# Stage borders of a two-layer decoder trunk: embedding, sums of squares, next layer's x, first loads

## What is computed

```
x += 1/2 * SwiGLU(RMSNorm(x))                        # ffn1, inner width 2816
x += W_out [ NSA | DiffAttn | HGRN2 ](RMSNorm(x) @ W_in)
x += 1/2 * SwiGLU(RMSNorm(x))                        # ffn2
x += sigmoid(RMSNorm(x) @ W_g) * RMSNorm(p[i] @ W_p) # p: per-layer embedding, width 256
SwiGLU(h) = (silu(h @ w_gate) * (h @ w_up)) @ w_down
```

## Time and profile before

| | us |
|---|---|
| median of 3 runs | 2407.98 |
| lowest, highest | 2405.62, 2409.56 |
| profiled execution | 2406.93 |
| its span, first to last instruction | 2405.1 |
| TensorE busy in it | 2292.6 |
| VectorE, ScalarE, GpSimd busy | 1208.7, 901.8, 82.5 |

### The profile page before, as it was taken

The page is one execution under the profiler, slowest core; times in us unless marked ns, Lnnn a source line. Parts: engine busy times, 40 slices in busy tenths (PEclk is TensorE's granted clock), DMA queues, the critical chain, the costliest instruction groups (busy, mean ns, idle before and its releaser), DMA issues. The chain is left out here.

```text
span 2405.1 us, 27598 instructions
## 1 busy us (share of the span) xinstructions
PE 2292.6 (95%) x10816; PEld 1806.7 (75%) x10816; DVE 1208.7 (50%) x1990; ACT 901.8 (37%) x1483; POOL 82.5 (3%) x119
## 2 busy tenths in 40 slices
PE   7999999899989999998989999998989899999988
PEld 5888887776656888887768888877766568888876
DVE  5444433466676444433554443345566764444335
ACT  5222223444654323222452322244455542222233
POOL 0000000032000000000000000001310000000000
PEclk9999999999999999999999999999999999999999
DMA  4433334212102333333223333343120023333322
GB/s 154 146 96 97 90 98 152 87 60 65 42 27 72 96 103 91 93 99 105 79 78 97 96 95 97 98 132 100 53 77 27 25 81 98 97 97 98 98 94 70
DMA packets 68986, 214.31 MB, mean 89 GB/s; under 512 B 8143, under 2 KB 15311, under 8 KB 68858
## 3 DMA queue, kind: packets, MB, share of 16 engines
q1 hardware_dynamic: 59344, 189.27, 26.1%
q10 hardware_dynamic: 9514, 23.27, 2.9%
HBM read 208.30 MB, written 5.40 MB: 89 GB/s over the span
## 5 line engine op out<-in xcount | busy, mean ns | idle before, releaser
L501 PE MATMUL main<-xh,wh 128*128 128x512 f32 x1944 | 781.5, 402 | 20.9 <-DVE xl L1407 19.7
L502 PE MATMUL main<-xl,wh 128*128 128x512 f32 x1944 | 763.2, 393 | 0.0
L503 PE MATMUL main<-xh,wl 128*128 128x512 f32 x1944 | 763.0, 392 | 0.0
L1400 DVE TENSOR_TENSOR wl<-raw,wh 128x1024 fp32r<-128x1024 f32 (+3 forms) x372 | 440.2, 1184 | 402.7 <-ACT wh L948 402.2
L948 ACT ACTIVATE wh<-raw 128x1024 fp32r<-128x1024 f32 (+3 forms) x372 | 378.1, 1017 | 499.6 <-PE main L503 465.4
L501 PEld LDWEIGHTS main<-xh,wh 128*128 128x128 f32 x1944 | 368.9, 190 | 128.0 <-issue 25.8
L502 PEld LDWEIGHTS main<-xl,wh 128*128 128x128 f32 x1944 | 369.1, 190 | 78.9 <-issue 5.5
L503 PEld LDWEIGHTS main<-xh,wl 128*128 128x128 f32 x1944 | 368.7, 190 | 78.6
L501 PE MATMUL main<-ffh,wh 128*128 128x512 f32 x704 | 273.9, 389 | 0.0
L502 PE MATMUL main<-ffl,wh 128*128 128x512 f32 x704 | 273.9, 389 | 0.0
L503 PE MATMUL main<-ffh,wl 128*128 128x512 f32 x704 | 273.9, 389 | 0.0
(11 more groups left out here) (230 smaller groups left out, 1937.8 us busy)
## 6 DMA issues: line engine op xcount, KB each, us to landing
raw<-in_ffn_gate SPq DMA_DIRECT2D x88, 512.0 KB, 3.6
raw<-in_ffn_up SPq DMA_DIRECT2D x88, 512.0 KB, 3.6
raw<-in_ffn_down SPq DMA_DIRECT2D x64, 448.0 KB, 3.3
raw<-in_w_in_t SPq DMA_DIRECT2D x40, 512.0 KB, 3.6
raw<-in_ffn_down SPq DMA_DIRECT2D x32, 512.0 KB, 3.5
raw<-in_wout SPq DMA_DIRECT2D x24, 384.0 KB, 3.1
w<-in_cmp_w ACTq DMA_DIRECT2D x16, 512.0 KB, 3.7
raw<-in_ple_gate SPq DMA_DIRECT2D x16, 512.0 KB, 3.2
```

The lines of the kernel that those rows point to most:

```text
L501: nc.tensor.matmul(out, lh, rh, start=start, stop=False, **kw)
L502: nc.tensor.matmul(out, lh, rl, start=False, stop=False, **kw)
L503: return nc.tensor.matmul(out, ll, rh, start=False, stop=stop, **kw)
L1400: nc.vector.tensor_tensor(wl[:, c % SLOTS, 0:n], raw[:, c % SLOTS, 0:n], wh[:, c % SLOTS, 0:n], ALU.subtract).then_inc(*tick("weights_lo", ...
```

## The change

1. The embedding is loaded into the FFN's gate buffer `fg` behind the last SiLU of ffn2, and is split during down product 3; its split form moves behind the FFN's buffers.
2. In both FFNs the sum of squares moves behind up product 0; one more chunk is split in tile 0, on ScalarE ahead of the factor.
3. "post" moves behind gate product 0 of the embedding stage; factor "ple" moves on ScalarE between output tiles 3 and 4; VectorE multiplies `emby` tile by tile within the loop over gate products.
4. In layer 0 the next layer's x is split tile by tile as the last gate product has read it (`x_read`): tiles 0 to 4 behind gate tile 6, tiles 5 to 7 behind gate tile 7.
5. At the start weight chunk 0 is loaded ahead of the table, the parameters behind chunk 2, and the line is copied behind tile 3.

```diff
@@ memory @@
+        embh, embl = sb("embh", [P, 2, SEQ], F32R), sb("embl", [P, 2, SEQ], F32R)
+        emb = fg
         place["at"] = region + (P - region) % 2048
-        emb = sb("emb", [P, 2, SEQ])
-        embh, embl = sb("embh", [P, 2, SEQ], F32R), sb("embl", [P, 2, SEQ], F32R)
@@ SyncE @@
-                sp.dma_start(onehot[0:33, :], a["onehot"]).then_inc(onehot_in, 16)
-                sp.dma_start(tab[0:BUCKETS, :], a["rel_bias"]).then_inc(onehot_in, 16)
...
                 load_ends(0)
-                load_params(0)
...
+                    if c == 0:
+                        sp.dma_start(onehot[0:33, :], a["onehot"]).then_inc(onehot_in, 16)
+                        sp.dma_start(tab[0:BUCKETS, :], a["rel_bias"]).then_inc(onehot_in, 16)
+                    if c == 2:
+                        load_params(0)
@@ TensorE @@
+                        if read and k < KT - 1:
+                            mm.then_inc(*tick("x_read", k))
...
+                        from_x((name + "_up", ft))
                         if ft == 0:
                             sum_squares(name)
-                        from_x((name + "_up", ft))
...
-                        sum_squares(("ple", "post")[h2])
+                        if h2 == 0:
+                            sum_squares("ple")
                     for dt in range(KT):
-                        from_x(("ple_gate", dt), "ple" if dt == 0 else None)
+                        from_x(("ple_gate", dt), "ple" if dt == 0 else None, read=dt == KT - 1 and layer < DEPTH - 1)
+                        if dt == 0:
+                            sum_squares("post")
@@ ScalarE, ffn @@
                             split(c + AHEAD)
                             if ft == 0:
+                                split(c + 1 + AHEAD)
                                 factor(name, rb[:])
...
+                    if name == "ffn2":
+
+                        act.dma_start(emb[:], a["p"][counts.layer]).then_inc(emb_in, 16)
                     for dt in range(KT):
...
                         square(nxt, dt, x[:, dt, :])
+                        if name == "ffn2" and dt == 3:
+                            act.wait_ge(emb_in, 16 * (counts.layer + 1))
+                            for k in range(2):
+                                nc.scalar.activation(embh[:, k, :], emb[:, k, :],
+                                                     ACT.Copy).then_inc(*tick("emb_hi", k))
@@ ScalarE, layers @@
+                def next_x(ks):
+
+                    counts.layer += 1
+                    for k in ks:
+                        if k < KT - 1:
+                            act.wait_ge(*done("x_read", k, layer=counts.layer - 1))
+                        else:
+                            act.wait_ge(*done("product", ("ple_gate", KT - 1), layer=counts.layer - 1))
+                        act.wait_ge(*done("x_new", "ple", k, layer=counts.layer - 1))
+                        split_x("ffn1", "ffn1", k)
+                    counts.layer -= 1
...
                     for dt in range(KT):
                         if dt % 4 == 0:
                             split(CHUNK[("ple_proj", dt // 4)] + AHEAD)
+                        if dt == 4:
+                            factor("ple", rb[:])
...
+                    split(CHUNK[("ple_gate", 0)] + AHEAD)
                     factor("post", rb2[:])
+                    if layer < DEPTH - 1:
+                        act.wait_ge(ends_in[layer + 1], 48)
                     for dt in range(KT):
                         split(CHUNK[("ple_gate", dt)] + AHEAD)
-                        if dt == 0:
-                            factor("ple", rb[:])
                         act.wait_ge(*done("pgate_scaled", dt))
                         nc.scalar.activation(pg[:, dt % 2, :], pg[:, dt % 2, :],
                                              ACT.Sigmoid).then_inc(*tick("pgate", dt))
+                        if layer < DEPTH - 1 and dt >= KT - 2:
+                            next_x(range(0, 5) if dt == KT - 2 else range(5, KT))
@@ VectorE @@
-                            split(c + AHEAD)
+                            split(c + AHEAD + (ft == 0))
...
-                    dve.wait_ge(*done("factor", "post"))
-                    for dt in range(KT):
-                        nc.vector.scalar_tensor_tensor(out=emby[:, dt, :], in0=emby[:, dt, :], scalar=col("post", dt),
-                                                       in1=rb2[:], op0=ALU.mult,
-                                                       op1=ALU.mult).then_inc(*tick("emb_normed", dt))
...
                         nc.vector.tensor_tensor(pg[:, dt % 2, :], bank_of(("ple_gate", dt))[:], rb[:],
                                                 ALU.mult).then_inc(*tick("pgate_scaled", dt, frees=("ple_gate", dt)))
+                        if dt == 0:
+                            dve.wait_ge(*done("factor", "post"))
+                        nc.vector.scalar_tensor_tensor(out=emby[:, dt, :], in0=emby[:, dt, :], scalar=col("post", dt),
+                                                       in1=rb2[:], op0=ALU.mult,
+                                                       op1=ALU.mult).then_inc(*tick("emb_normed", dt))
...
+                        if layer < DEPTH - 1 and dt >= KT - 2:
+                            next_x(range(0, 5) if dt == KT - 2 else range(5, KT))
```

More of the change, by code:

```diff
@@ L508, in chunk, with from_x @@
                     return wh[:, c % SLOTS, 0:n], wl[:, c % SLOTS, 0:n]
-                def from_x(key, stage=None, at=None, order=tuple(range(KT))):
+                def from_x(key, stage=None, at=None, order=tuple(range(KT)), read=False):
                     out = take(key, 0, at)
@@ L1344, in _ @@
                     at["logs"] = False
[L1345 to L1351, removed]
+                    if layer == 0:
+                        act.wait_ge(ends_in[layer], 48)
+                        for k in range(KT):
                             act.wait_ge(x_in[k], 16)
-                        split_x("ffn1", "ffn1", k)
-                        if k < AHEAD:
-                            split(k)
+                            split_x("ffn1", "ffn1", k)
+                            if k < AHEAD:
+                                split(k)
                     split(AHEAD)
@@ L1364, in _ @@
                     ffn("ffn2", "ple", "ple")
[L1366 to L1369, removed]
                     for dt in range(KT):
@@ L1521, in ffn @@
                         add_square(nxt, dt)
+                        if name == "ffn2" and dt == 3:
+                            for k in range(2):
+                                dve.wait_ge(*done("emb_hi", k))
+                                nc.vector.tensor_tensor(embl[:, k, :], emb[:, k, :], embh[:, k, :],
+                                                        ALU.subtract).then_inc(*tick("emb_lo", k))
                 def scaled(name, out):
@@ L1914, in mixed_lo, with next_x @@
                                             ALU.subtract).then_inc(*tick("x_lo", "mixed", k))
+                def next_x(ks):
+                    counts.layer += 1
+                    for k in ks:
+                        split_x("ffn1", "ffn1", k)
+                    counts.layer -= 1
                 for layer in range(DEPTH):
                     counts.layer = layer
[L1918 to L1927, removed]
+                    if layer == 0:
+                        for k in range(KT):
+                            if k < AHEAD:
+                                split(k)
+                            split_x("ffn1", "ffn1", k)
+                            if k == 3:
+                                dve.wait_ge(line_made, 1)
+                                nc.vector.tensor_copy(line[0:BIAS_HEADS, 0:SEQ],
+                                                      bank_of("line0")[0:BIAS_HEADS, :]).then_inc(
+                                                          *tick("line_copied", 0, frees="line0"))
+                                nc.vector.tensor_copy(line[0:BIAS_HEADS, SEQ:LINE],
+                                                      bank_of("line1")[0:BIAS_HEADS, 0:P]).then_inc(
+                                                          *tick("line_copied", 1, frees="line1"))
                     split(AHEAD)
@@ L1936, in _ @@
                     ffn("ffn2", "ple", "ple")
[L1937 to L1940, removed]
                     for dt in range(KT):
```

## The result

The changed kernel takes 2366.67 us (median of 4 runs, 2365.19 to 2371.97), the kernel before 2408.77 beside it (2405.62 to 2411.61): ratio 0.9828, 95% interval 0.9815 to 0.9842. The forecast was 2370.6 in a range of 2364 to 2379. Its profiled execution took 2371.97 us, of which 2370.2 span.

What follows compares the result with a forecast made beforehand. TensorE was taken to bound all but some 50 us, at the borders; gains of 6.5 (start), 11.2 and 11.7 (embedding borders) and 8.0 (layer border) sum to 37.4, giving 2370.6 us, range 2364 to 2379.

Steps and rivals of the forecast that it cites:

- the embedding border: End of second FFN to first embedding-gate product, twice: 19.7 us warm, 20.4 with clock; gains 11.2 and 11.7 us.
- the new stall: Embedding border: TensorE waits 1.7 us before gate product 0 for the bank freed by ScalarE's copy of output tile 4.
- The hidden part: Embedding border: the squares of "post" end at 1153.8, behind gate product 0 until 1154.55, hidden by 0.7 us.
- The table load: ScalarE, factor "ple" at the embedding border: load costs 1.28 us, without the skill page's added drain of about 1.38 us.
- Layer border: Layer 0's end to layer 1's first up product: 15.3 us against 23.37, gain 8.0, with stalls of 2.2 and 1.1 us.
- The wait for acc: Layer border: TensorE stalls 1.1 us behind the up product until the additions of squares end.
- The start: First gate matmul to the sum of squares' end: 29.9 against 36.43 us, gain 6.5, ends 4 and 8.5.
- I take 0.4 us off it: The start: weight chunk 1, landing at 13.43 before, is taken to land 0.4 us earlier.
- FFN entries: Squares behind the up product at four entries: the later factor is covered; second FFN's two entries gain 0.
- rival D: Slower than before: lag after FFN entries delays weights in 84 gate-up pairs; 2421 us at 0.6 us each; chance 0.03.
- C: Short stalls keep the clock low, 2.3 us at each of three places, start at its low end: 2378.3 us; chance 0.15.
- B: No new stalls at the embedding and layer borders: 2360.7 us, about 2364 with one of them left; chance 0.12.

Runs made afterwards that it cites:

- The two undone versions: Changed kernel with the embedding loaded and split only after ffn2: 2386.77 us; changed kernel with squares "post" back ahead of gate product 0: 2376.99 us.
- the second profile: The changed kernel run again unaltered, beside the kernel with three further edits: median 2370.34 us, profiled execution 2364.24 us.
- the version with three more edits: Changed kernel with factor ple behind the embedding output's squares, layer 0's chunk 1 behind all x tiles, layer 1's behind the early tiles: 2366.29 us.
- the undone kernels: Changed kernel with one part undone each: FFN squares 2385.43 us, early x split 2372.59, early embedding load 2386.77, "post" squares 2376.99.

## Why the prediction was right, and where it was off

**What bounds, and the embedding border: right.** The warm sum of 19.74 was met to 0.04 us in both layers, down to the new stall: it is shown with 1.34 and costs 1.6 in the window (19.75 against 18.11 without it), where 1.7 was reckoned. The hidden part was right too: the squares of "post" never wait. The 0.7 us for the clock were not needed: after so short a stall the clock stayed at 1.00. The two undone versions give the parts: early load 8.0, "post" 4.8, together 12.8 against 11.9. They don't add up because the slow matmuls don't: TensorE is busy for 18.4 us of the border in the changed kernel, 19.9 with the embedding late, 21.0 with "post" back and 21.5 with both, as before.

**The table load: the row was right.** The load starts 1142.63 and the logarithm 1143.92, 1.29 us later. The Trainium skill ("ScalarE: Activation LUTs", What ACT_TABLE_LOAD costs) adds a drain of about 1.38 us, which does not show here either. With it the stall would have been an estimated 2.7 us.

**Layer border: right in mechanism, two small errors.** The order on VectorE, the wait at tile 5 (2.2 reckoned, 2.01 shown) and its tile are as forecast. The wait for acc, put at 1.1 (the prediction's own 1218.5 and 1219.4 give 0.9), appears only where the clock stays up (0.70); in both profiles of the changed kernel slower matmuls fill it, for 0.4 us more than the 0.3 allowed. What the prediction did not say is how the two edits share the gain: the squares carry 6.1 us (23.37 to 17.29) and the split of x 1.6; the split of x alone brought the additions 1.5 us forward and the border nothing (23.36), as slow matmuls took as much.

**The start: the term that was mis-sized.** 6.5 forecast, 8.26 measured. The step that failed is "I take 0.4 us off it" for the landing of chunk 1: it came 1.6 us earlier, which is 1.2 of the 1.7 us. The other 0.5 is the clock: triples 1 to 7 were reckoned at 7.5 us (16.06 to 23.6) and took 7.0 (14.84 to 21.85), with the last three at full clock. In the second profile the shares are the other way round: chunk 1 came 1.2 us earlier, the triples took 6.3 us. The parameters moved behind the chunks account for 0.6 to 1.3 us of the landing by their experiment; for the table no share is shown. That TensorE's first triple (12.1 instead of 14.4) has no heir was right, and the version that lets it have one, with chunk 1 behind the tiles of x, gains 0.7 us of the 2.7 between the triples.

**FFN entries and rival D: right.** The later factor leaves nothing behind (348.18 against 348.16), and the entries move by +1.71 and -0.59, which is the clock, for the waits end at the same distance from the first matmul. Without the edit the layer 0 entry is 14.30, with it 16.05, but the changed kernel's second profile has one of each sort too (15.87 and 14.29).

**C** (the clock stays down behind each short stall) held at one of the three places and in part (0.7 us at the layer border, not 2.3). **B** described the version with three more edits at the embedding border.

The median came 3.9 us under the forecast: 1.7 from the start, 1.3 from the clock not lost at the embedding borders, less 0.4 at the layer border. That these partly cancel is luck; the remaining 1.3 us are inside what executions differ by.

## What to carry to other kernels

A border between two stages is a race of in-order queues: write down, for the engine that bounds, when each queue will have delivered, in the order of its program, and the next stall comes out to some tenths of a microsecond, as did the windows of the undone kernels, except for the slow matmuls behind a stall: those cost up to 1.5 us more than reckoned. A reduction over a stage's whole output belongs behind the next product that doesn't need it; ahead of it, an earlier split of the data gained nothing here, and behind it 1.6 us. Judge edits of this size by windows of the profile cut at the same matmuls, since totals of one kernel differ by more than the edits give.

## What the runs showed of the hardware

The time of one and the same kernel follows the granted clock of its execution: the kernel before 2402.57 us at 0.984 and 2416.94 at 0.977, the changed one 2364.24 at 0.989 and 2371.97 at 0.984. Within an execution the same stall does not always cost the same: the entry of ffn2 took 14.27 to 16.86 us in the ten profiles, each time with a first wait of 2.07 or 2.08, and 15.87 and 14.29 within one of them. Stalls of 3.6 to 5.4 us ahead of a sum of squares were followed by 1.5 to 3.0 us of time lost to matmuls at 1.2 GHz, one of 3.6 us by 1.6 in the kernel before and by 2.8 with "post" put back; stalls of 1.3 us cost 0.3 beyond themselves, at a granted clock of 1.00. Why a given stall brings the clock down and another doesn't is left open.

The table load took 1.28 us on ScalarE, and the function that needs it began 0.01 us later.
